# A transformer pair of blocks in fp32 on one core: gate projections of the first branch moved into the latent attention heads

## The reference, cut to what matters

```python
for l in range(DEPTH):
    h = x @ w_in[l]
    c_q, c_kv, k_pe, dq, dk, dv, mq, gate_pre = jnp.split(h, splits, axis=-1)
    o_mla = _mla_branch(c_q, c_kv, k_pe, ...)       # 8 latent heads
    o_diff = _diff_branch(dq, dk, dv, ...)          # 8 heads
    o_mem = _mem_branch(mq, mem, mem_w_kv[l])       # 4 heads
    g = jax.nn.sigmoid(gate_pre.reshape(b, s, N_BRANCH, d) + b_gate[l])
    wb = w_branch[l]
    merged = (g[:, :, 0] * (o_mla @ wb[:MLA_OUT])
              + g[:, :, 1] * (o_diff @ wb[MLA_OUT:MLA_OUT + DIFF_OUT])
              + g[:, :, 2] * (o_mem @ wb[MLA_OUT + DIFF_OUT:]))
    x = _layernorm(DEEPNORM_ALPHA * x + merged @ w_out[l], ln1_g[l], ln1_b[l])
    f = jnp.square(jax.nn.relu(x @ mlp_w1[l])) @ mlp_w2[l]
    x = _layernorm(DEEPNORM_ALPHA * x + f, ln2_g[l], ln2_b[l])
```

## Time and profile before

| | |
|---|---|
| median of 3 runs | 4189.98 us (4186.84, 4189.98, 4192.81) |
| span of the profiled execution | 4189.2 us |
| granted TensorE clock, mean | 0.968 |
| latent heads, first layer 2.x | 2017.29 to 2127.70 us |
| from there to the scores of `diff_pe` | 2127.70 to 2198.18 us |
| latent heads, second layer 2.x | 3127.34 to 3238.09 us |

### The profile page before, as it was taken

One profiled execution on the slowest core, in us unless ns is written; L12 is line 12 of the kernel. 1 busy time (PEld: TensorE's weight loads), 2 busy tenths in 40 slices (PEclk: granted clock), 3 DMA queues, 4 the chain that ended last, 5 costly groups with the idle time before them and its releaser, 6 DMA issues.

```text
span 4189.2 us, 59665 instructions
## 1 busy us (share of the span) xinstructions
PE 3968.2 (95%) x20860; PEld 3354.5 (80%) x20860; DVE 2070.7 (49%) x3364; ACT 1490.1 (36%) x2420; POOL 1630.0 (39%) x2044
## 2 busy tenths in 40 slices
PE   7999988999988979999999999999989999999998
PEld 6788888999977767888777788788877777887887
DVE  5556655223347666225737723533367476235225
ACT  3212222111236543222646534322246456333222
POOL 1111123333421105566333245466642423555565
PEclk9899999999989989999999999999999999999999
DMA  5334211112110002322121122223221211322222
GB/s 187 125 123 144 79 51 51 61 65 64 61 46 26 21 11 93 98 98 96 56 70 57 51 86 96 76 96 100 96 66 41 81 51 61 100 86 77 99 95 96
DMA packets 92747, 328.31 MB, mean 78 GB/s; under 512 B 10240, under 2 KB 12544, under 8 KB 92544
## 3 DMA queue, kind: packets, MB, share of 16 engines
q1 hardware_dynamic: 90928, 323.61, 23.3%
q10 hardware_dynamic: 1616, 1.90, 0.2%
HBM read 323.38 MB, written 2.10 MB: 78 GB/s over the span
## 4 chain that ended last, share of the span: by engine, by line
issue 61%; POOL 30%; PE 8%; DVE 1%; POOLq 1%; ACT 0%; DVEq 0%
POOL Wl L259 30%; PE psum L1142 3%; PE psum L1143 3%; PE psum L1144 3%; POOLq L254 0%; POOLq L256 0%; DVE S L1990 0%; DVE M L2168 0%; PE psum L1209 0%; DVE X L1990 0%; DVE X L2124 0%; PE psum L1199 0%; DVE X L2185 0%; POOLq L259 0%; ACT hand L380 0%
## 5 line engine op out<-in xcount | busy, mean ns | idle before, releaser
L259 POOL TENSOR_TENSOR Wl<-raw,Wh 128x256 fp32r<-128x256 f32 x2040 | 1629.8, 829 | 2552.9 <-ACT Wh L370 2552.5
L370 ACT ACTIVATE Wh<-raw 128x1024 fp32r<-128x1024 f32 x510 | 540.0, 1059 | 1689.9 <-PE psum L1144 1664.3
L1142 PE MATMUL psum<-Hh,Wh 128*128 128x512 f32 (+1 forms) x2704 | 1037.9, 384 | 50.2 <-DVEq L2033 17.0
L1143 PE MATMUL psum<-Hl,Wh 128*128 128x512 f32 (+1 forms) x2704 | 1018.3, 377 | 0.0
L1144 PE MATMUL psum<-Hh,Wl 128*128 128x512 f32 (+1 forms) x2704 | 1017.0, 376 | 0.0
L1142 PE MATMUL psum<-Gh,Wh 128*128 128x512 f32 (+3 forms) x2032 | 751.1, 370 | 17.5 <-DVEq L2033 7.9
L1144 PE MATMUL psum<-Gh,Wl 128*128 128x512 f32 (+3 forms) x2032 | 745.7, 367 | 0.0
L1143 PE MATMUL psum<-Gl,Wh 128*128 128x512 f32 (+3 forms) x2032 | 745.3, 367 | 0.0
L1142 PEld LDWEIGHTS psum<-Hh,Wh 128*128 128x128 f32 x2704 | 520.5, 192 | 157.6 <-issue 52.1
L1144 PEld LDWEIGHTS psum<-Hh,Wl 128*128 128x128 f32 x2704 | 520.1, 192 | 71.4
L1143 PEld LDWEIGHTS psum<-Hl,Wh 128*128 128x128 f32 x2704 | 521.0, 193 | 67.9 <-issue 1.3
(11 more groups left out here) (345 smaller groups left out, 4702.9 us busy)
## 6 DMA issues: line engine op xcount, KB each, us to landing
raw<-in_wstream SPq DMA_DIRECT2D x510, 512.0 KB, 3.4
stage<-in_ada SPq DMA_DIRECT2D x80, 512.0 KB, 4.3
M<-in_ada SPq DMA_DIRECT2D x16, 512.0 KB, 5.9
X<-in_xT SPq DMA_DIRECT2D x1, 2048.0 KB, 14.1
out<-X SPq DMA_DIRECT2D x8, 256.0 KB, 2.0
X<-in_ctxT SPq DMA_DIRECT2D x1, 1024.0 KB, 9.2
M<-in_memT ACTq DMA_DIRECT2D x1, 1024.0 KB, 5.6
M<-in_axial ACTq DMA_DIRECT2D x1, 512.0 KB, 3.5
```

What stands on the lines that cost most here:

```text
L259: pool.tensor_tensor(Wl[:, s, c], raw[:, s, c], Wh[:, s, c].bitcast(F32), ALU.subtract).then_inc(w_low, 1)
L370: act.activation(Wh[:, s], raw[:, s], ACT.Copy).then_inc(v["w_high"], 1)
L1142: pe.matmul(dst, a[0], b[0], start=first, stop=False)
L1143: pe.matmul(dst, a[0], b[1], start=False, stop=False)
```

## The change

In heads 0 to 6 PE makes gate tile h between `keys_and_values()` and `turned_values(h)`; head 7 makes tile 7 where it made tile 0; the tile behind `output()` of head 7 is gone. ACT takes each tile in `raw_gate`: it adds the bias and writes the sum to `M` (SBUF), frees the bank itself, and converts a weight block; the conversion that stood at the end of the head now stands behind the raw values. The sigmoids are made in place in `M`, four behind `high_output(7)` and four behind `high_twin(1)`. `branch(0)` has product tiles only: DVE waits for `gates_made` and multiplies the product into `M`. The weight stream is put in the new order.

```diff
@@ second_act
-    latent_act(act, v, tiles, from_bank, next_weights, gate_from, gate, diff_counts)
-    branch(0, True, True)
+    latent_act(act, v, tiles, from_bank, next_weights, diff_counts)
+    for m in range(0, KT, 2):
+        used(2)
@@ latent_act
+    def raw_gate(m):
+
+        b = tiles.look(act)
+        at = LVEC["b_gate"] + m
+        act.activation(v["M"][:, m * SEQ:(m + 1) * SEQ], psum[:, b, :], ACT.Identity,
+                       bias=v["lvec"][:, at:at + 1]).then_inc(v["bank_free"][b], 1)
+        next_weights()
+
+    def gates(ms):
+
+        for m in ms:
+            g = v["M"][:, m * SEQ:(m + 1) * SEQ]
+            act.activation(g, g, ACT.Sigmoid).then_inc(v["gates_made"], 1)
...
         exps(2 * h + 1)
         if not more:
-            gate(0, 0)
+            raw_gate(h)
         if before:
             high_output(h - 1)
         if more:
             tiles.skip(1)
             keys_and_raw_values(h + 1)
+            next_weights()
+            raw_gate(h)
         high_values()
         if more:
             high_queries()
         for qt in range(4):
             high_weights(qt)
-        if more:
-            next_weights()
     take_twin(3)
     high_output(7)
-    gate(0, 1)
+    gates(range(KT // 2))
     tiles.skip(2)
     high_values()
     high_twin(0)
     high_twin(1)
+    gates(range(KT // 2, KT))
@@ latent_pe
             rotated(2 if before else 3)
             keys_and_values()
+            from_tokens()
         else:
             pe.wait_ge(v["raw_done"], counts.raw_done.next())
         turned_values(h)
@@
     from_tokens()
     output()
-    from_tokens()
     twin_rotated(0)
     twin_rotated(1)
@@ branch (PE)
-        if not begun:
+        if gated and not begun:
             for _ in range(2):
                 project_block(H, X_SEGS)
@@ dve_program
+            for m in range(KT):
+                b = look()
+                dst = M[:, m * SEQ:(m + 1) * SEQ]
+                dve.wait_ge(v["gates_made"], KT * l + m + 1)
+                tt_last(b, dst, psum[:, b, :], dst, ALU.mult)
+                if m == 1:
+                    twin_operands()
@@ weight_blocks
         for h in range(8):
             yield padded(...)
             if h == 0:
                 yield twin(0, 1)
+            else:
+                yield block(w_in, gate0 + (h - 1) * P)
+        yield block(w_in, gate0 + (KT - 1) * P)
```

More of the change, by code:

```diff
@@ L200, in build @@
         keys_scaled = sem("keys_scaled")
+        gates_made = sem("gates_made")
         spread_done, squared = sem("spread_done"), sem("squared")
@@ L834, in attention_act, with latent_act @@
     high_output(3, 1, 1)
-def latent_act(act, v, tiles, from_bank, next_weights, gate_from, gate, counts):
+def latent_act(act, v, tiles, from_bank, next_weights, counts):
     psum, X, stage, soft, S0 = (v[n] for n in ("psum", "X", "stage", "soft", "S0"))
@@ L1482, in _ @@
             tools = tiles, weights, project, project_block, wait_ready, mm3, psum, v["tile_done"]
-            branch(pe, tools, H, G, True, lambda: None)
+            branch(pe, tools, H, G, True, lambda: None, gated=False)
             last_spread = diff_pe(pe, v, tiles, weights, project_block, mm3, exact, diff_counts)
@@ L1924, in memory_pe, with branch @@
             turned_values()
-def branch(pe, tools, H, G, paired, between=None):
+def branch(pe, tools, H, G, paired, between=None, gated=True):
     tiles, weights, project, project_block, wait_ready, mm3, psum, tile_done = tools
@@ L2657, in low_sums, with branch @@
                                       ALU.subtract).then_inc(v["for_pe"], 1)
-            def branch(n, begun, beside=None):
+            def branch(n, begun):
                 for m in range(0, KT, 2):
@@ L2677, in branch @@
                             free(gates[j])
-                    if beside and m == 0:
-                        beside()
                     if n == 2 and m == 4:
@@ L2682, in branch @@
                         low_sums(OUT_ORDER[:2])
-            begun, twin_operands = latent_dve(dve, v, look, free, do, tt, tt_last, ts, (sinM, cosM, sinD, cosD), root_q,
-                                              lambda: inverse_roots(root_q), gate, for_pe, diff_counts)
-            branch(0, begun, twin_operands)
+            twin_operands = latent_dve(dve, v, look, free, do, tt, tt_last, ts, (sinM, cosM, sinD, cosD), root_q,
+                                       lambda: inverse_roots(root_q), tiles.skip, for_pe, diff_counts)
+            for m in range(KT):
[5 more added lines that the diff above has]
+                    twin_operands()
             begun = diff_dve(dve, v, look, free, do, tt, tt_last, ts, stt, (sinD, cosD), neg_lam, gain, gate, for_pe, diff_counts)
@@ L2866, in attention_dve, with latent_dve @@
     low_output(3, 1, 1)
-def latent_dve(dve, v, look, free, do, tt, tt_last, ts, tables, root_q, query_roots, gate, for_pe, counts):
+def latent_dve(dve, v, look, free, do, tt, tt_last, ts, tables, root_q, query_roots, skip, for_pe, counts):
     psum, stage, soft, S0, S1 = (v[n] for n in ("psum", "stage", "soft", "S0", "S1"))
@@ L2994, in latent_dve @@
     raw_queries()
-    begun = []
     for h in range(8):
@@ L3005, in latent_dve @@
         if not more:
-            begun.append(gate())
+            skip(1)
         if before:
@@ L3025, in latent_dve @@
     low_values()
-    return begun, twin_operands
+    return twin_operands
 def diff_dve(dve, v, look, free, do, tt, tt_last, ts, stt, tables, neg_lam, gain, gate, for_pe, counts):
@@ L3337, in weight_blocks @@
         yield twin(0, 0)
+        gate0 = 672 + 3072 + 512
         for h in range(8):
@@ L3341, in weight_blocks @@
                 yield twin(0, 1)
-        gate0 = 672 + 3072 + 512
+            else:
+                yield block(w_in, gate0 + (h - 1) * P)
+        yield block(w_in, gate0 + (KT - 1) * P)
         def branch(i, rows, paired):
             for m in range(0, KT, 2):
-                for j in range(2):
+                for j in range(2 if i else 0):
                     yield block(w_in, gate0 + i * D + (m + j) * P)
@@ L3349, in branch @@
                     yield block(wb, (m + j) * P, rows, 2 * P if paired else P)
-        first = branch(0, slice(0, 512), True)
-        yield next(first)
         yield twin(0, 2)
-        yield from first
+        yield from branch(0, slice(0, 512), True)
         for h in range(1, 8):
```

7 lines of the change are left out of this document (2 added, 5 removed).

## The result

| | before | after |
|---|---|---|
| median of 4 runs | 4189.02 us | 4220.9 us |
| lowest to highest | 4186.84 to 4192.81 us | 4218.79 to 4222.87 us |
| span of the profiled execution | 4189.2 us | 4221.1 us |
| mean granted clock of TensorE | 0.968 | 0.963 |

The ratio of the times is 1.0072, 95% interval 1.0059 to 1.0084: the change makes the kernel about 32 us slower. The prediction was 4191.9 us, no difference, with a range of 4185 to 4200.

The account below looks back on a forecast made before the run. TensorE, busy 95%, was taken as the bound, so only its waits count. Per layer -0.29 + 0.78 + 0.14 - 0.4 + 0.7 = +0.9 us, both layers +1.9: span 4191.1, median 4191.9 us, range 4185 to 4200.

Parts of the forecast that it names:

- part 1: Heads 0 to 6: gap put behind the gate block; per layer heads 1 to 6 lose 0.78 us, head 0 wins 0.29.
- The chain: Head's end, from raw_gate's start over conversion, Vh, Vl and Ql to the next scores: 3.90 us, against 3.77 before.
- the gaps are filled: Rival, chance 0.06 in whole or part: PE loses its idle time in the heads, 4170 us; half of it, 4178.
- part 2: Heads 0 to 6: Ql beside POOL takes 0.02 us longer each, at most 0.42; 0.14 us a layer.
- the second rival: POOL holds Ql, chance 0.07: Ql waits for a whole POOL subtraction in 14 heads, 4201.8 us; for all four, 4211.
- The rival's own case: Within the second rival: Ql waits for all four POOL subtractions, 1.4 us a head, 4211 us; rival's chance 0.07.
- part 3: Head 7: Gh can start when the output tile is done; wins 0.4 us a layer, between nothing and 0.5.
- part 4: Behind head 7: third product block waits for its converted weights, 0.7 us a layer, between nothing and 2.3.
- the third block: Third product block of the first branch, behind head 7: its weights come late, 0.7 us taken per layer.
- part 5: DVE in the branch loses waits for handed sigmoids and multiplies in M directly: nothing, PE's banks come back in time.

Follow-up runs that it names:

- experiment 2: Changed kernel with the conversion behind raw_gate moved to the head's end and an equally long ScalarE copy, feeding nobody, in its old place: 4206.56 us.
- experiment 8: The kernel of experiment 2 with five matmuls nobody reads before the last tile of turned weights: 4194.38 us.
- experiment 1: Changed kernel with the weight conversion behind raw_gate moved to the head's end, behind the weights' high parts: 4179.16 us.
- experiment 3: Changed kernel with matmuls nobody reads in both waits of heads 0 to 6, five before the last turned tile, two before the scores: 4198.8 us.
- experiment 5: Kernel before, no gate block moved, with a ScalarE copy of 1024 columns feeding nobody in front of Vh in heads 0 to 6: 4206.96 us.
- experiment 4: Changed kernel with the conversion at the head's end, turned_values before the gate block and raw_gate behind high_queries: 4158.97 us.
- experiment 7: Changed kernel with only the wait before the scores filled, by two matmuls nobody reads: 4206.61 us.
- experiment 6: Changed kernel with only the wait before the last turned tile filled, by five matmuls nobody reads: 4201.03 us.

## Why the prediction was wrong

- **What the gap is made of, and whether the gate block fills it** (part 1): right. The gate block leaves the wait where it was, behind itself. The chain is the forecast's, spacing by spacing, and without POOL it gives 19.48 us a head against 19.46 (experiments 2 and 8). The rival "the gaps are filled" had its condition right too: with Vh not behind the conversion it gave 4179, forecast 4178.
- **Ql beside POOL** (part 2): the term was mis-sized. I took 0.02 us, the row of the same operation in a similar place; it is 0.51 us each time, 7 us in both layers instead of 0.3. It went past the high end I gave it (0.42) and past the 0.46 from which the second rival was to count. Read one by one, POOL's subtractions of the earlier trace rows show that the row I chose, 0.71 us, did contend, but began only 0.17 us before the running one ended; the 1.11 beside it began 0.56 us before such an end. Ql in the changed kernel begins 0.65 us before one. In all three the operation ends 0.55 us behind the end of POOL's subtraction, and so in the other kernels where Ql runs beside POOL (1.19 to 1.25 us, with 0.65 to 0.70 left, or with the next subtraction just beginning). The forecast had Ql 3.16 - 1.73 = 1.43 us behind POOL's first subtraction, so at the start of the third, and with this reading of the earlier trace rows the price would have come out at some 0.5 us. The Trainium skill (SBUF — State Buffer, Who interferes with whom) says that a DVE instruction with two SBUF inputs contends with a GpSimd instruction that reads SBUF, and that the later one is blocked for the whole instruction of the other. The trace agrees for Ql: 0.69 us without POOL and 1.20 beside it. The rival's own case, all subtractions waited for (1.4 us a head), did not come for Ql, but it came in head 0, for a product that I had not costed at all.
- **Head 0** (part 1): forecast to win 0.29 us. At full clock and with its old wait it is 18.06 us against 17.6, and 0.51 of that are Ql; the 0.29 were right. But it lost another 3 us in each layer: 1.4 from the small product beside POOL and 1.6 from the clock behind the wait of 2.1 us. Nothing in the trace of before announces this but the product's own 0.63 us beside POOL against 0.16 alone, rows that I did not read. Had the tie come out as before, the changed kernel would be 6 us faster, some 4215.
- **Head 7** (part 3): right in the first layer, -0.37 us for -0.4. In the second it was longer before (15.13 us); without the clock it would have won 0.7 (14.46 us in experiments 1 and 3), but it lost 1.6 with it (16.01).
- **Behind head 7** (part 4): the third block was 0.14 and 0.48 us late for 0.7. The sigmoids are 0.55 and not 0.60 us each, and POOL ran undisturbed. With small losses at other blocks what stands behind head 7 loses 0.4 and 0.7 us, 1.1 for a forecast of 1.4.
- **DVE** (part 5): right, nothing waits for it in the branch.
- **The step that failed** is one that the sum never names: it adds waits to stretches in which the granted clock was 1.00 and takes the same clock for what follows. In the trace of before PE waited 0.97 + 0.21 us at each end of a head without losing it; I lengthened the wait and priced only the wait. It measured 1.32 + 0.72 us, and matmuls behind it ran at half speed after 9 of 14 heads (and in both heads 0, behind their own wait), for 22.2 us. Experiment 3 takes this away by filling the wait; experiment 5 makes it in the old kernel. No rival spoke of it, so the range ended 21 us short of the result.

By size, in the two layers from head 0 to `diff_pe`, where the forecast was +1.9 us and the trace has +33.4: clock 22.2 us, Ql 2 x 7 x 0.49 = 6.9, head 0's wait 2.8, the rest of the chain 0.2, head 7 -0.3, behind it -0.3; together 31.5 us, which is the whole of 33.4 - 1.9. The rest of the kernel was 1.5 us shorter in this execution; by the medians the forecast is 4220.9 - 4191.9 = 29.0 us short.

The rival of the filled gaps was priced too low: 4170 us if all idle time went, but experiment 4 measured 4159, since PE's busy time hides part of what a wait costs.

What stays open is the exact rule of the clock (which head loses it, and for how long), and the spread of the runs in kernels that lose it only sometimes. Neither was followed through repeated profiles of one kernel.

## What to carry to other kernels

A wait of TensorE has two prices: its length, and what the matmuls behind it lose if the clock falls; where a change lengthens or merges waits in a dense stretch, a rival with the slow matmuls belongs in the sum, worked out from a stretch of the same trace at the lower clock. Before filling a gap with moved work, look where on the other engines the released operation stands: here Vh, behind a conversion that nobody needed yet, and a later conversion (or values before tokens) turned a loss of 32 us into a gain of 10 or of 30. Where a moved conversion brings GpSimd beside a VectorE operation with two SBUF inputs, don't take over a duration from another place: work out how much of GpSimd's running instruction is left when the operation begins, and add it.

## What the runs showed of the hardware

- TensorE's clock fell behind waits of 1.32 us with 0.21, 0.26 or 0.72 us more at the end of a head of some 20 us that was otherwise dense (8, 3 and 9 of 14 ends in experiments 2 and 7 and in the changed kernel), behind 1.05, 0.26 or 0.35, and 0.21 us in the old kernel (2 of 14, experiment 5), and behind each of nine single waits of 2.1 us in heads 0. It did not behind 0.85 to 1.05 and 0.21 us (before), 0.38 and 0.21 (experiment 1), nor 0.17 and 0.74 us (experiment 6), in 14 ends each. Matmuls of 512 columns then start 0.43 us apart instead of 0.23, and each fall cost 1.6 or 3.2 us. The Trainium skill (TensorE: Matmul & The Clock Gate, A second HAM failure mode: psum-queue depth-cycling) tells of another kernel in which frequent short idle times between groups of matmuls made the clock go back and forth between its levels. The trace agrees, with waits for banks and operands at a head's end.
- Matmuls whose result nobody reads, put into a wait, made the kernel faster than it was without them, by 22 us, or 19.3 us once head 0's wait is left out (experiment 3).
- A VectorE subtraction with two SBUF inputs (0.69 us alone) that began beside a GpSimd subtraction ended 0.55 us behind the end of that one: 0.71, 1.11 and 1.20 us with 0.17, 0.56 and 0.65 us left. The GpSimd subtraction behind it took 1.18 instead of 0.73 us.
- A VectorE product of 128x2 elements took 0.16 us alone and 2.01 us beside GpSimd, ending when the last of eight back-to-back GpSimd subtractions ended; in 13 of 22 heads 0 it took 0.63 us at a distance the same within 0.01 us, ending with the one that was running. The wait can go over one GpSimd instruction or over several, and which it is did not follow from the program.
